# In every slot of the expert stage GpSimd issues the gather of output rows ahead of the gather of the next pair's input rows

## The reference, cut to what matters

```python
# 8 heads, 16 picks each, out of 128 x 128 experts; T = 256 tokens
eidx = e1 * PEER_KEYS + e2                    # (T, 8, 16) expert numbers
gate = softmax(sc)
u  = take(u_emb, eidx)                        # one input row of 2048 f32 for each pick
a  = einsum('cd,chkd->chk', h, u)
w  = gate * gelu(a)
vv = take(v_emb, eidx)                        # one output row of 2048 f32 for each pick
out = einsum('chk,chkd->cd', w, vv)
```

## Time and profile before

| | |
|---|---|
| median of the three runs | 1929.18 us |
| lowest, highest | 1928.41, 1930.54 us |
| time of the profiled execution | 1930.08 us |
| span in it, first to last instruction | 1928.3 us |
| busy: TensorE, VectorE, GpSimd, ScalarE | 88%, 66%, 48%, 26% |
| bytes by the gathers' queue / SyncE's queue | 450.02 / 163.57 MB |
| mean granted TensorE clock | 0.93 |

### The profile page before, as it was taken

The page is one execution under the profiler, slowest core; times in us unless marked ns, Lnnn a source line. Parts: engine busy times, 40 slices in busy tenths (PEclk is TensorE's granted clock), DMA queues, the critical chain, the costliest instruction groups (busy, mean ns, idle before and its releaser), DMA issues.

```text
span 1928.3 us, 31074 instructions
## 1 busy us (share of the span) xinstructions
PE 1696.0 (88%) x12212; PEld 1134.9 (59%) x12212; DVE 1271.6 (66%) x2449; ACT 509.6 (26%) x981; POOL 926.4 (48%) x712
## 2 busy tenths in 40 slices
PE   6999989999999999978888888888788988988855
PEld 5988878888998888845555554554343322322200
DVE  4536788887555469877587787878899444454521
ACT  6623556565534431122222222321000000000100
POOL 2022223332153024766565665657687755646662
PEclk9999999999999999989999999999555999999968
DMA  4578779988655759999999999999999999999998
GB/s 190 169 167 182 182 168 209 213 198 197 239 177 194 267 194 342 364 411 412 400 389 408 397 397 399 414 388 384 411 391 378 382 406 418 407 414 413 385 383 324
DMA packets 125905, 615.36 MB, mean 319 GB/s; under 512 B 31160, under 2 KB 31160, under 8 KB 60088
## 3 DMA queue, kind: packets, MB, share of 16 engines
q0 software_dynamic: 96768, 450.02, 64.9%
q1 hardware_dynamic: 29008, 163.57, 23.2%
HBM read 750.76 MB, written 2.10 MB: 390 GB/s over the span
## 4 chain that ended last, share of the span: by engine, by line
PE 39%; DMA 38%; DVE 9%; issue 8%; POOL 5%; ACT 1%; POOLq 0%; DVEq 0%; ACTq 0%; SPq 0%
DMA uv<-v_tab,eidT 21%; DMA uv<-u_tab,eid 15%; PE ps L1836 5%; DVE uv L1702 4%; PE ps L2174 4%; POOL uv L638 3%; PE ps L1753 3%; PE ps L1754 3%; PE ps L1755 3%; POOL uv L657 2%; PE ps L1841 2%; PE ps L2248 2%; DMA parts<-W 2%; PE ps L1843 2%; PE ps L1842 2%
## 5 line engine op out<-in xcount | busy, mean ns | idle before, releaser
L1702 DVE CUSTOM_DVE_ANT_0 uv<-uv,xn 128x2048 f32<-128x2048 f32 x256 | 586.3, 2294 | 307.2 <-DMA uv<-u_tab,eid 268.0
L657 POOL DMA_INDIRECT uv<-v_tab,eidT x256 | 432.7, 1690 | 203.0 <-PE ps L2174 115.9
L638 POOL DMA_INDIRECT uv<-u_tab,eid x256 | 314.6, 1229 | 346.8 <-DVE av L1702 140.8
L2174 PE MATMUL ps<-uv,late 128*32 128x512 f32 x2048 | 322.8, 710 | 175.2 <-DMA uv<-v_tab,eidT 162.3
L2203 PE MATMUL ps<-h2T,ring 128*128 128x256 f32 x1024 | 253.5, 392 | 0.0
L2174 PEld LDWEIGHTS ps<-uv,late 128*32 128x32 f32 x2048 | 46.7, 115 | 319.2 <-DMA uv<-v_tab,eidT 265.0
L2203 PEld LDWEIGHTS ps<-h2T,ring 128*128 128x128 f32 x1024 | 193.0, 199 | 26.0 <-issue 3.4
L1017 ACT ACTIVATE ring<-ps 128x512 f32<-128x512 f32 x128 | 76.3, 596 | 348.2 <-PE ps L2196 295.9
L1118 DVE TENSOR_TENSOR low_ring<-ring,wh 128x2048 fp32r<-128x2048 f32 x43 | 101.1, 2353 | 74.6 <-ACT wh L689 74.5
L606 POOL DMA_DIRECT2D parts<-W x80 | 70.4, 879 | 151.3 <-ACT parts L807 123.5
L987 ACT ACTIVATE ga<-av,st 128x16 f32<-128x16 f32 x16 | 4.9, 307 | 465.8 <-DVE av L1702 465.7
(11 more groups left out here) (363 smaller groups left out, 3081.1 us busy)
## 6 DMA issues: line engine op xcount, KB each, us to landing
ring<-W SPq DMA_DIRECT2D x61, 1024.0 KB
parts<-W POOLq DMA_DIRECT2D x160, 320.0 KB, 5.6
ring<-u_tab SPq DMA_DIRECT2D x32, 1024.0 KB
ring<-v_tab SPq DMA_DIRECT2D x32, 1024.0 KB
ring<-W SPq DMA_DIRECT2D x40, 384.0 KB, 5.4
xn<-x SPq DMA_DIRECT2D x4, 1024.0 KB, 7.9
uv<-u_tab,eid POOLq DMA_INDIRECT x256
uv<-v_tab,eidT POOLq DMA_INDIRECT x256
```

Source lines behind the costliest of these rows:

```text
L638: pool.indirect_dma_start(rows_to, None, u_tab, bass.IndirectOffsetOnAxis(ap=eid[:, p, i:i + 1], axis=0), bounds_check=E0 * NK - 1, oob_is ...
L657: pool.indirect_dma_start(rows_to, None, v_tab, bass.IndirectOffsetOnAxis(ap=eidT[:, p, r:r + 1], axis=0), bounds_check=last, oob_is_err=F ...
L1702: nc.vector.tensor_tensor_reduce(rows_in, rows_in, xn[:, T, :], 1.0, 0.0, ALU.mult, ALU.add, av[:, p % 2, i:i + 1]).then_inc(s_dot, 1)
L2174: ins = nc.tensor.matmul(ps[32 * n:32 * n + 32, j, :], zd[:, p % 2, 32 * r:32 * r + 32], rows_in[:, n * 512:(n + 1) * 512], start=(p == 4 ...
```

## The change

The two calls of the loop change places; nothing in the two functions, in the waits or in any other engine's program changes.

```diff
             for p in range(PAIRS + 1):
                 for i in range(PICKS):
+                    if p:
+                        output_rows_of(p - 1, i)
                     if p < PAIRS:
                         input_rows_of(p, i)
-                    if p:
-                        output_rows_of(p - 1, i)
                     if p == 0 and i == 8:
                         pool.wait_ge(s_wdone, RING + W_PQ + 3)
                         pool.memset(zd[:, :, :], 0.0).then_inc(s_zero, 1)
```

## The result

The changed kernel takes 1956.93 us (median of five runs, 1954.95 to 1962.93) against 1929.11 us, a ratio of 1.0145 with an interval of 1.0126 to 1.0164: 28 us slower, where 1941 us, 12 us slower, was forecast with 1953 us as the upper end. The profiled execution took 1957.72 us with a span of 1955.9 us, 27.6 us more than the span of before.

What follows compares the result with a forecast made beforehand. The prediction took DMA transfers to bound the kernel. Its terms, 2.3 + 7.0 + 2.5 + 1.0 + 1.0 - 1.5 = +12.3 us on the median of 1929.18, gave 1941 us, range 1926 to 1953.

Steps and rivals of the forecast that it cites:

- What bounds the stage: Expert stage between starts of rounds: DMA transfers set its length, share 1.00 to 1.01; order acts only on their idle moments.
- Inside a round: Between starts of rounds: each input gather only shifts one place back against the outputs, hidden by the transfers, 0 us.
- Second round: Start of second round: input gather 32 waits behind output gather 0 and the DMA engines miss one gather, +2.3 us.
- Third to eighth round: Starts of these rounds: input gather (p, 0) lands later, input gather (p, 4) waits behind output gather (p-1, 4); 0 to 4.56 us each.
- The sizes between the bounds: Starts of rounds: third and fourth 3.5 us each, fifth 2.5, sixth 1.0, seventh and eighth 0.5 each.
- One sign named for the fourth: Starts of rounds three and four: the DMA share was to fall below 0.8 over 10 us.
- seventh and eighth: Starts of these rounds: share 1.02 and 1.01, dense loads in a second queue can fill the hole, +1.0 us together.
- Last round: Last round: one gather more is in the queue in the hole of 1.1 us, -1.5 us, bounds -2.28 and +2.28.
- The upper bound of 4.56 us: Each start of rounds three to eight: at most two gathers of 2.28 us of DMA time lost.
- full price: Rival, starts of rounds: every start costs its 4.56 us, +32 us, 1961 us; chance 0.08 for it or near it.
- the queue that holds: Rival, starts of rounds: eight gathers in flight are enough cover, about 1931 us, no change; chance 0.22.
- the faster kernel: Rival, slots before each start of a round: outputs first feeds the queue sooner, -5.5 us, 1923.7 us; chance 0.14.

Runs made afterwards that it cites:

- the experiment on slots 8 to 27: Kernel before, with outputs first only in slots 8 to 27 of rounds 3 to 9: ratio 1.0023, +4.4 us.
- the kernel with the weights ahead: Changed kernel, with the weights of pair p-1 computed on VectorE ahead of its wait for input gather (p, 0): 1936.25 us, ratio 1.0026.
- the two halves: Kernel before, with outputs first in rounds 3 to 9 only in slots 0 to 3 (ratio 1.0060), or only in slots 4 to 31 (1.0068).
- a second profile: Changed kernel, with TensorE doing two more slots' dense products ahead of the first pick of the seventh and eighth rounds: ratio 1.0108.
- a lead of -2: Input gathers one place later than in the changed kernel, which has a lead of -1: ratio 1.0370 to the kernel before.

## Why the prediction was wrong, point by point

**What bounds the stage** was right: the DMA share between the starts is still 1.00 to 1.01 in the three stretches shown, and 22.4 of the 27.6 us are idle time of the DMA engines. (One reading was loose: the last of the slices in the earlier trace rows is at eight tenths, not nine.)

**Inside a round: 0.** Not borne out in full: the experiment on slots 8 to 27 gave +4.4 us (1.9 to 7.1), the kernel with the weights ahead leaves some 2 us for it. Whether the order or that experiment's seams cost it is open.

**Second round: +2.3.** Agrees with 2.9 us alone (1.0 to 5.0); the share fell from 0.58 to 0.45, which is 1.3 us over those 10 us.

**Third to eighth round: the mechanism** (later input gather 0 through dot, weights and pick; input gather 4 behind that wait; two equal parts) was right, shown by the two halves and by the weights moved ahead. **The sizes between the bounds failed, and the more so the fuller the queue had been held to be.** By the table, which is good to some 2 us for one start: second and third together, put at 5.8, came to 4.5; the fourth, put at 3.5, to 5.2; the fifth, put at 2.5, to 5.5; the sixth, put at 1.0, to 0.9, which fits cover by VectorE but doesn't show it (a second profile had 2.5, and with a lead of -2 this stretch was the dearest). One sign named for the fourth, a share below 0.8 over 10 us, didn't come: it was 0.84.

**The step that failed most is "seventh and eighth (1.02, 1.01), where the dense loads come in a second queue and can fill the hole: 0.5 each".** They came to 5.1 and 4.7 in the changed kernel, which is 8.8 us of the 15.3 missed, and to 6.8 us together (4.2 to 9.1) where they alone were changed. Two readings were at fault. First, a share of 1.0 says that the queue isn't empty, not how much is in it; the shares fell to 0.66 and 0.75, so it held less than the change takes away. Second, the other queue isn't independent: its loads wait for the engine that waits, in one case 18.5 us. The rule of the Trainium skill cited there (DMA: Bandwidth & Descriptors, Queues, rings and completion order) speaks of queues for which the engine has work; the sum by it would have been still lower, and no run contradicts the rule itself, since once TensorE kept freeing places the share rose to 0.92 and 0.98.

**Last round: -1.5.** Not shown either way. The changed kernel's profile has +1.3 and another 0.5 up to the end, the one with only the seventh and eighth round changed has -1.4; but the one with only the second round changed has -2.5 at the same point, where its order is that of the kernel before, so readings of this size are scatter.

**The upper bound of 4.56 us** a start was passed by some tenths in the table, which is within its scatter. One thing that the bound leaves out is in the rows: at the fourth, fifth, seventh and eighth start the pick on which everything waits takes 1.93 or 1.94 us in place of 1.06. Added to the bound this would give 4.56 + 0.9 = 5.4 us, an estimate from these rows that no run tested. The rival named "full price", +32 us with a chance of 0.08, came nearest with 28, though not in all its parts: the sixth start paid 0.9. The range, up to 1953, left it out. The other two, the queue that holds and the faster kernel, fall with the 28 us.

## What to carry to other kernels

Where two streams of transfers share one in-order queue and the users of one wait now and then for the users of the other, keep the stream that is waited for ahead, and look at the seams between rounds, not at the average: here one place of order cost some 5 us at a seam and at most some 4 us inside all the rounds together. A full DMA share isn't a reserve, and a second queue is one only if its own releases don't come from the stalled engine. When the bounds of a term are 0 and a full price and the reserve can't be read, put more chance on the full price.

## What the runs showed of the hardware that was not expected

TensorE's clock. In the kernel before, the first pick of the seventh round and the dense products behind it are

```profile
1552.11 1.06 PE L2174 MATMUL ps<-uv,late 128*32 128x512 f32 x8 [1.53 <-DVE late L1617]
1552.99 3.62 PE L2248 MATMUL ps<-ring,late 128*32 128x512 f32 x32
```

and the window there shows the full 2.4 GHz (1.00). In the changed kernel, after a wait of 7.12 us, the window shows 0.73, the pick took 1.94 us, and the 32 dense products 5.71 us, which is the lower level of 1.2 GHz for some us. With dense products put into the wait the window is at 1.00 again and the pick takes 1.04 us. The other starts agree: waits of 2.17, 0.36 and 1.53 us at the fourth, fifth and eighth before, with picks of 1.06 us, and of 6.18, 7.19 and 5.32 us after, with picks of 1.93 or 1.94 us; at the third the pick took 1.75 us before already, behind a wait of 3.77 us. So behind a longer wait TensorE's own work took longer as well; what that alone added to the kernel's time wasn't told apart.
